# An expert gather ring of eight buffers in place of ten, and a weight slot that keeps two query pieces, then two output pieces

## What is computed

```python
def _peer(x, w_pq, sub_keys, u, v):
    q = (xt @ w_pq).reshape(T, PEER_HEADS, 2, PEER_HALF)
    scores = jnp.einsum('thcd,hckd->thck', q, sub_keys)
    ...   # top 16 of each half, top 16 of the 256 sums, per head: 8 * 16 = 128 experts a token
    def block(args):
        u_sel = jnp.take(u, idb, axis=0)          # 128 rows of 1024 for each token
        h = jax.nn.gelu(jnp.einsum('td,ted->te', xblk, u_sel), approximate=False)
        v_sel = jnp.take(v, idb, axis=0)
        return jnp.einsum('te,ted->td', gb * h, v_sel)
```

## Time and profile before

| what | value |
|---|---|
| median of 3 runs (lowest to highest) | 2794.46 us (2789.7 to 2795.59) |
| profiled execution | 2794.93 us |
| its span from first to last instruction | 2793.1 us |
| TensorE busy / DVE / ACT / POOL, share of the span | 90% / 62% / 35% / 24% |
| gathers, first issue to last issue | 134.7 to 1569.6 us |
| bytes moved by DMA | 800.03 MB, 536.93 of them by the gathers |
| granted TensorE clock, mean | 0.982 |

### The profile page before, as it was taken

One profiled execution on the slowest core, in us unless ns is written; L12 is line 12 of the kernel. 1 busy time (PEld: TensorE's weight loads), 2 busy tenths in 40 slices (PEclk: granted clock), 3 DMA queues, 4 the chain that ended last, 5 costly groups with the idle time before them and its releaser, 6 DMA issues.

```text
span 2793.1 us, 29435 instructions
## 1 busy us (share of the span) xinstructions
PE 2508.8 (90%) x9845; PEld 1561.3 (56%) x9845; DVE 1737.3 (62%) x3951; ACT 974.6 (35%) x2020; POOL 665.7 (24%) x635
## 2 busy tenths in 40 slices
PE   7989888798887899887877899999999999999999
PEld 3544444364442565432322356885688668875787
DVE  1678866755758666667776457653566556546664
ACT  1225322234222354222221234442444444424543
POOL 0044433433434334434444201001000020002000
PEclk9999999999999999999999999999999999999999
DMA  7299999999999999999999732544054325533352
GB/s 290 107 407 421 412 421 418 421 421 413 408 421 422 416 394 393 420 415 422 421 421 418 314 122 84 202 148 198 34 213 175 131 83 184 193 117 121 144 188 104
DMA packets 112145, 800.03 MB, mean 286 GB/s; under 512 B 13123, under 2 KB 15766, under 8 KB 19606
## 3 DMA queue, kind: packets, MB, share of 16 engines
q0 software_dynamic: 73760, 536.93, 46.6%
q1 hardware_dynamic: 38262, 261.60, 24.7%
HBM read 797.41 MB, written 1.07 MB: 286 GB/s over the span
## 4 chain that ended last, share of the span: by engine, by line
PE 63%; DMA 24%; DVE 7%; issue 3%; ACT 2%; SPq 1%; POOL 0%; DVEq 0%; ACTq 0%
PE psum L1343 15%; DMA weights<-in_peer_uv,scratch 13%; PE psum L1451 13%; PE psum L1074 11%; DMA arena<-in_peer_uv,scratch 9%; PE psum L1408 8%; PE psum L1410 4%; PE psum L1160 3%; PE psum L1168 2%; DVE heads_arena L2269 2%; PE psum L1146 1%; PE psum L1057 1%; PE psum L1135 1%; PE psum L1122 1%; ACT scratch L1781 1%
## 5 line engine op out<-in xcount | busy, mean ns | idle before, releaser
L1343 PE MATMUL psum<-weights,scratch 128*128 128x512 f32 x1232 | 589.4, 625 | 146.7 <-ACT scratch L1781 146.5
L2774 POOL DMA_INDIRECT weights<-in_peer_uv,scratch x308 | 356.0, 1156 | 608.4 <-PE psum L1343 503.3
L1343 PEld LDWEIGHTS psum<-weights,scratch 128*128 128x128 f32 x1232 | 234.1, 198 | 472.2 <-issue 249.6
L1343 PE MATMUL psum<-arena,scratch 128*128 128x512 f32 x816 | 383.3, 614 | 78.3 <-ACT scratch L1781 78.2
L2618 DVE TENSOR_TENSOR piece<-weights,piece 128x2048 fp32r<-128x2048 f32 x128 | 292.1, 2292 | 181.4 <-ACT piece L1860 181.4
L1074 PE MATMUL psum<-weights,xT 128*128 128x512 f32 (+2 forms) x792 | 338.2, 581 | 25.5 <-DMA weights<-in_w_qkv_a 15.2
L1451 PE MATMUL psum<-piece,hidden 128*128 128x512 f32 x1536 | 358.9, 390 | 0.0
L1773 ACT ACTIVATE scratch<-scratch 128x2 f32<-128x2 f32 x256 | 51.9, 203 | 844.0 <-DVE heads_arena L2269 843.8
L1408 PE MATMUL psum<-split_x,piece 128*128 128x512 f32 x896 | 318.6, 398 | 0.0
L1451 PEld LDWEIGHTS psum<-piece,hidden 128*128 128x128 f32 x1536 | 284.3, 188 | 59.6
L1343 PEld LDWEIGHTS psum<-arena,scratch 128*128 128x128 f32 x816 | 152.4, 194 | 286.2 <-issue 159.1
(11 more groups left out here) (266 smaller groups left out, 2779.1 us busy)
## 6 DMA issues: line engine op xcount, KB each, us to landing
weights<-in_w_up SPq DMA_DIRECT2D x64, 1024.0 KB, 4.9
weights<-in_w_down SPq DMA_DIRECT2D x64, 1024.0 KB, 4.8
weights<-in_w_kv_b SPq DMA_DIRECT2D x16, 1024.0 KB, 9.0
weights<-in_peer_w_q SPq DMA_DIRECT2D x12, 1024.0 KB, 9.1
weights<-in_a_w_in SPq DMA_DIRECT2D x6, 2048.0 KB, 10.2
weights<-in_w_q_b SPq DMA_DIRECT2D x8, 1024.0 KB, 9.4
weights<-in_w_o_b SPq DMA_DIRECT2D x8, 1024.0 KB, 9.2
weights<-in_a_w_out SPq DMA_DIRECT2D x4, 2048.0 KB, 8.9
```

Source lines behind the costliest of these rows:

```text
L1343: mm = pe.matmul(psum[g.bank][:, :], diagonal[:, n % DIAGONALS, :], row[:, D + half * BANK:D + (half + 1) * BANK], start=(k == 0), stop=(k ...
L2774: pool.indirect_dma_start(gathered[n % GATHER_SLOTS], None, rows, bass.IndirectOffsetOnAxis(ap=expert[:, w % NT, k:k + 1], axis=0), elemen ...
```

## The change

The ring has eight buffers. Weight slot 3 is no longer part of it. It holds, one after the other, what the kernel has in it anyway and another chunk of the same size. The first is `peer_chunks[1]`, columns 512 to 1023 of the first layer's query weight, which is loaded before the gathers begin, for tile 0. `Second` now uses its two halves in pairs 49 and 50 of pass 0 in place of two pieces of its own (`KeptPiece`). The other is `kept_o`, the first 512 columns of `w_o_b`, 2 MB, loaded once in pass 1 behind the layer norm's gains and used in pairs 35 and 36 of passes 1 and 2. The remaining two output pieces of these passes stay pieces of slot 0. `early_in` exchanges the slots of its chunks 1 and 2, so that chunk 1 goes to slot 3.

```diff
-GATHER_SLOTS = 10
+GATHER_SLOTS = 8
...
-        in_slot = {slot: [weights[:, slot, n * ROW:(n + 1) * ROW] for n in range(2)] for slot in (1, 2, 3)}
-        gathered = in_slot[2] + in_arena + in_slot[1] + in_slot[3]
+        in_slot = {slot: [weights[:, slot, n * ROW:(n + 1) * ROW] for n in range(2)] for slot in (1, 2)}
+        gathered = in_slot[2] + in_arena + in_slot[1]
...
-                self.loaded = 16 * half_uses[self.half]
+                self.landed = (piece_loaded[self.half], 16 * half_uses[self.half])
...
+        class KeptPiece:
+            def __init__(self, c, n, bank):
+                self.landed = (c.sem, c.loaded)
+                self.view = c.halves[:, n]
+                self.group = group(bank)
...
-                self.peer_q = [Piece(src, n, 2 + n % 2) for n, src in enumerate(column_pieces(A["peer_w_q"][0], 0))]
+                self.peer_q = [Piece(src, n, 2 + n % 2) for n, src in enumerate(column_pieces(A["peer_w_q"][0], 0)[0:2])]
+                self.peer_q += [KeptPiece(peer_chunks[1], n, 2 + n) for n in range(2)]
...
-                self.o = [Piece(src, first + n, banks[n % 2]) for n, src in enumerate(column_pieces(A["w_o_b"][0], 0))]
+                self.o = [KeptPiece(kept_o, n, banks[n]) for n in range(2)]
+                self.o += [Piece(src, first + n, banks[n]) for n, src in enumerate(column_pieces(A["w_o_b"][0], 0)[2:4])]
...
-        ring_free = {0: diff_out_blocks[1][-1], 2: later_blocks[4][-1], 4: later_blocks[5][-1], 6: later_blocks[1][-1], 8: peer_q[1]}
+        ring_free = {0: diff_out_blocks[1][-1], 2: later_blocks[4][-1], 4: later_blocks[5][-1], 6: later_blocks[1][-1]}
...
+        kept_o = in_weights(A["w_o_b"][0], 0, 3, second.peer_q[3].group)
...
-        for slot, buffers in ((1, (6, 7)), (2, (0, 1)), (3, (8, 9))):
+        kept_until = stick[1].o[1].group
+        slot_release[3] = (psum_filled[kept_until.bank], kept_until.filled)
+        for slot, buffers in ((1, (6, 7)), (2, (0, 1))):
...
-        early_in = TileProjection(chunks_laid_out(A["a_w_in"][0], A_IN), (0, 2, 3, 1), (0, 1, 2, 3))
+        early_in = TileProjection(chunks_laid_out(A["a_w_in"][0], A_IN), (0, 3, 2, 1), (0, 1, 2, 3))
...
-            load_stick(second.peer_q[2:])
             scored = second.scores[3]
...
                 load_ln(2 if s.t == 0 else 4)
+                if s.t == 0:
+                    load_chunks([kept_o])
                 load_stick(s.pieces[2:])
-                load_stick(s.o)
+                load_stick(s.o[2:])
```

More of the change, by code:

```diff
@@ L1150, in piece_loaded_to @@
             def piece_loaded_to(c):
-                pe.wait_ge(piece_loaded[c.half], c.loaded)
+                pe.wait_ge(*c.landed)
                 bank_free(c.group)
```

## The result

| | median us | lowest to highest | profiled execution | its span |
|---|---|---|---|---|
| before | 2794.76 (4 runs) | 2789.7 to 2795.59 | 2794.93 | 2793.1 |
| after | 2819.66 (4 runs) | 2814.35 to 2820.68 | 2820.68 | 2818.9 |

After is to before as 1.0081, with a 95% interval of 1.0064 to 1.0099. The kernel became 0.8% slower, 24.9 us by the medians. I had forecast 2797.3 and a range up to 2808, so the time lies 12 us above the range.

The account below looks back on a forecast made before the run. DMA was taken to bound most of the first 1600 us, with short stretches set by TensorE or DVE. Terms 2.0 + 1.8 + 1.6 + 5.0 - 4.0 - 1.9 - 1.7 = +2.8 us gave 2797.3, range 2786 to 2808.

Parts of the forecast that it names:

- part 1: Two buffers fewer: gathers late only where old issue of n + 2 plus 5.5 us passes n's old landing; clean stretches lose zero.
- five places: Where the release test failed: start, pair 34 and pair 55 of pass 0, and the output pieces of passes 1 and 2.
- Start of pass 0: Gather 8 lands up to 3.6 us late, a DMA gap behind it takes up part; +2.0 us.
- Pair 34: Pass 0, behind the norm's steps on DVE: a gather 2.0 us late; +1.8 us, ends 0 and 2.0.
- Query pieces and pair 55: Pass 0: 5.0 us of DMA from two unloaded pieces is spent by the smaller ring; +1.6 us, ends -5.0 and +2.0.
- The kept chunk: Output chunk loaded early in pass 1, near pair 7, where DMA is full; +5.0 us, other end 0.
- Output pieces of pass 1: Two pieces not loaded; 4.7 of 5.0 us can be had, less the query pieces' share; -4.0 us, ends -5.0 and -2.0.
- Pass 2: Two output pieces not loaded; 2.6 us to be had, less late gathers and a query piece; -1.9 us, ends -5.0 and 0.
- Last pass: No added delay: clean stretch stays at 421 GB/s, with issue to landing 9.1 us in place of 14.1.
- Chunk 1: Next input projection's chunk, issued when the last gather lands, 9 us before, removes TensorE's wait; -1.7 us.
- the bytes count in full: Rival: 4 MB fewer fetches save 10.0 us and the ring costs nothing, 2782.8; half or more of it, chance 0.18.
- The starving ring: Rival: clean pairs starve too if a gather behind one other needs over 8.3 us; 2800 and up, chance 0.32.

Follow-up runs that it names:

- ring9: The kernel before with nine gather buffers in place of ten and nothing else; 2799.11 us, ratio 1.0010.
- ring8: The kernel before with eight gather buffers, slot 3 empty during the gathers, all query and output pieces loaded as before; 2825.11 us, ratio 1.0105.
- after_weigh_first: The kernel after with VectorE weighing pair i - 1 before the products of pair i, and ScalarE's diagonals moved ahead likewise; 2789.95 us, ratio to before 0.9971.
- ring6: The kernel before with six gather buffers, one execution; 3286.44 us.
- ring10_hold8: The kernel before with all ten buffers, but GpSimd waits for the mix of gather n - 8 before issuing gather n; 2823.59 us, ratio 1.0086.
- the kernels with the new order: Pair i - 1 weighed ahead of pair i's products: kernel after 2789.95 us, kernel before 2790.49, eight buffers without kept pieces 2793.06, nine with half a slot kept 2786.54.
- after_late_kept: The kernel after with the 2 MB output chunk loaded behind the twelve pieces of pass 1, some 28 pairs later; 2819.99 us, ratio 1.0099.
- ring8_output: The kernel after with the output pieces kept but all query pieces loaded as before; 2821.54 us, ratio 1.0082.

## Why the prediction was wrong, step by step

The forecast was +2.8 us on the profiled execution, and it became +25.8. Of the 23.0 us between, 4.0 arose in pass 0, 2.7 in pass 1, 8.3 in pass 2, 1.6 in the last pass and 6.4 behind the last pass's gathers (chunk 1 included).

The failing step is the test of part 1, "old issue of n + 2, plus 5.5, against the old landing of n", and the sentence that it fails in five places. It went wrong in two ways.

First, I had run it only where I was looking. Over all 512 gathers of the kernel before, the same test with the same 5.5 us fails for 53. Beside my places it fails in pairs 34 to 37 of pass 1, by up to 1.7 us, and in pairs 23 to 39 of pass 2, by up to 6.2. I had no term for these, and put pass 2 at -1.9 where it was +6.4.

Second, 5.5 us is the landing of a gather with nothing ahead, and the test takes the releases at their old times. At my five places, the gathers of the kernel after that it was meant for took 5.7 us (start of pass 0), 6.2 (pair 34), 8.6 and 10.8 (the two of pair 55), 9.0 and 7.9. So the floor was about right at the first two, and 2.4 to 5.3 us too short at the other three. At the two places where I counted on a saving that ate 3.5 of the 4.7 us to be had in pass 1, and 2.4 of the 2.6 in pass 2.

The other half of part 1, "in clean stretches DMA stays full", held for this kernel (420 GB/s, 5.04 us a pair), though not for the same ring without the kept pieces; that stands under the last pass below.

How thin the reserve became can be counted. Every 0.1 us from the first mix to 30 us before the last I took how many gathers were between the start of their issue and their last completion signal, and summed the bytes of all DMA packets in those times. Each cell has the us and, where these are ten or more, the GB/s:

| in flight | before | ring9 | ring8 | after | after_weigh_first | ring6 |
|---|---|---|---|---|---|---|
| 1 | 1 | 2 | 14, 238 | 15, 283 | 5 | 431, 202 |
| 2 | 23, 381 | 58, 358 | 145, 372 | 176, 359 | 46, 369 | 999, 340 |
| 3 | 88, 385 | 195, 393 | 708, 407 | 672, 408 | 208, 396 | 412, 367 |
| 4 | 184, 407 | 655, 417 | 532, 415 | 528, 418 | 483, 416 | 17, 356 |
| 5 | 633, 419 | 475, 420 | 33, 421 | 31, 423 | 526, 420 | 0 |
| 6 and 7 | 471, 421 | 24, 423 | 0 | 0 | 126, 422 | 0 |
| lost against 421.5 GB/s (us) | 22 | 30 | 56 | 56 | 30 | 509 |

The kernel before spent 1104 of its 1400 us at five or more in flight; the kernel after spends 31 there and 863 at three or fewer. (The ring of six also had 35 us with none.) Fewer in flight and a lower rate go together: five or six have 419 to 423 GB/s, three 367 to 408, two 340 to 381, one 202 to 283. But the number alone doesn't set the rate. At three it is 385 in the kernel before and 408 after, and in pairs 10 to 40 of the last pass the kernel after had three or four in flight and 417 at either. Where few are in flight because TensorE frees no buffer, the low rate is the consequence of a wait and not its cause.

The last row is the sum of (421.5 - rate) / 421.5 over all the time. It is a restatement and no test: it equals the time counted less the bytes divided by 421.5, so its differences are how much longer a kernel took, plus the bytes that it saved. Ring 8 loses 34 us more than before by it and is 29.6 late; the rest comes from where the count begins and ends: the kernel before has 1.5 MB more inside it, and ring 8 starts its first mix 1.7 us earlier. A test would forecast one kernel from another. Shifting the time before by two gathers, with its own rates (ring 8's for one in flight), adds some 130 us, where two buffers cost 30; shifting it by one adds some 40, where one buffer cost 3 to 4. So the distribution shows that the reserve is gone, not what that costs. What it costs is shown by ring10_hold8 and the kernels with the new order.

The time of a gather by what was ahead of it at its issue gives the size of the second error. In the kernel after it is 6.5 us at the median with one gather ahead (17 of them), 8.3 with two (89) and 9.1 with three (344). In the ring of six, with none ahead, it is 5.9 (45). The Trainium skill, "DMA: Bandwidth & Descriptors", section "Anatomy of one DMA", has a fixed 2.0 us for a DMA issued from GpSimd and puts most of it behind the last byte. In the ring of six the first packet of a gather with nothing ahead started 1.9 us after its issue did, so here that much lies ahead of the first byte, and the measurement decides. The formula of the Trainium skill there makes an estimate of 4.4 us for the whole gather, which would have made my sum still smaller; the shortest landing in the ring of six was 5.3.

Now term by term, at the mixes of the kernel after:

- **Start of pass 0, predicted +2.0: +4.0 at pair 10**, beyond the upper end of 3.6. The test was near for the first gather: number 8 went out at 158.97, took 5.7 us and landed 3.0 later than in the kernel before. But the DMA gap behind it, which I had counted on to take up a part, grew instead: 349 GB/s at 160 to 180 us in place of 372. Once late, the gathers stayed late. The chain there has one that was released at 176.44 and took 13.1 us, as it took 13.4 in the kernel before, since the pass's pieces are loaded just then:

```profile
176.19 0.26 issue
176.44 13.08 DMA weights<-in_peer_uv,scratch
189.53 0.02 issue
189.55 1.25 DVE heads_arena L2283 x2
```

  I had taken the same pieces as a reason for the lower half. They didn't help; the gathers share DMA with them in both kernels.
- **Pair 34, predicted +1.8: from +4.3 at pair 33 to +6.4.** Right in place and near in size; +3.9 was the level from pair 26 to 30, so up to 2.5.
- **Query pieces and pair 55, predicted +1.6: +3.9**, from 5.5 at pair 47 to 9.4. I had seen that the 5.0 us of the saved loads would be lost, and the stretch at 314 GB/s shows it. The lateness at pair 55 was more than twice what the test gave: its two gathers took 8.6 and 10.8 us from their issue, with two and three ahead of them, and not 5.5.
- **The kept chunk, predicted +5.0: +5.3 at pair 9 of pass 1.** Right in size. The step is gone in after_late_kept and back in ring8_output, which has the early load (+6.0 from pair 7 to 9). But ring8, without that load, went 3.2 us later there in its one profiled execution, so a part can be the ring.
- **Output pieces of pass 1, predicted -4.0: -1.2** from pair 34 to the end. With ten buffers the saved loads brought 6.4 us in this pass; with eight the ring took most of it. This was the first large error: the earlier trace rows show when the gather could be released, but it took 9.0 us from there, with two gathers ahead, in place of 5.5.
- **Pass 2, predicted -1.9: +6.4.** Of this +4.1 arose between pairs 29 and 34, and +4.0 between pairs 46 and 55, of which 1.4 went back by the last pair. The first is where the test fails by up to 6.2 us and I hadn't looked. Two things of 1.7 to 1.8 us each can be read there. The mix of pair 30 took 5.40 us in place of 3.70, in a stretch with a granted clock of 0.91. And pair 34 waited for a gather that a late mix released:

```profile
1090.55 5.40 PE psum L1357 x8
...
1098.54 1.73 PE psum L1357 x4
1100.27 0.26 issue
1100.53 1.90 POOL weights L2788
1102.43 0.30 issue
1102.73 7.61 DMA weights<-in_peer_uv,scratch
```

  The sign that I had named came: the gap at 1040 to 1110 us is wider. The stretches of 20 us from 1040 had 391, 363, 381 and 423 GB/s before, and 379, 376, 365 and 380 after.
- **Last pass, predicted 0: +1.6.** Nearly right for this kernel; the chain has the 9.1 us that I forecast. Yet the same ring lost 5.6 us here in ring8 and 9.1 in ring10_hold8. In both, stretches with a low granted clock have low DMA rates (0.84 with 379 GB/s at 1360 us in ring8, 0.83 with 359 at 1340 in ring10_hold8). The kernel before has such a stretch too, and there DMA stays full. From 1320 to 1340 us, first the kernel before, then ring8; the last three columns are the granted clock, DMA's share and GB/s:

```profile
1320.00:1340.00 20.00, 15.30 (x31) 6.04 (x30) 15.85 (x45) 7.50 (x18) 7.77 (x8) 0.91 1.01 420
1320.00:1340.00 20.00, 16.00 (x33) 6.33 (x32) 16.01 (x40) 7.07 (x18) 10.22 (x8) 0.91 1.00 390
```

  So "clean stretches stay full" holds with eight buffers only as long as nothing delays a mix; with ten, a mix may be 1.7 us late and DMA doesn't show it. The low clock isn't why the kernel after is slower as a whole: from its first mix to its last the granted clock has a mean of 0.974, and 0.971 in the kernel before.
- **Chunk 1, predicted -1.7: -2.0**, from +21.2 at the last mixes to +19.2. Right; TensorE goes on without a wait:

```profile
1613.58 7.03 PE L1614 MATMUL psum<-heads_arena,const 128*128 128x512 f32 x16
1620.45 7.03 PE L1088 MATMUL psum<-weights,xT 128*128 128x512 f32 x16
```

- **Behind that, predicted 0: +6.6 in the profiled execution**, in five steps, one of -1.6 and four of +0.9 to +2.9. The two nearest follow the granted clock. The kernel before had 0.91 at 1620 to 1640 us, where it lost 1.6 us to the kernel after; the kernel after has it later. First the one row of the kernel before, then two of the kernel after:

```profile
core 0: us, PE busy (x) PEld busy (x) DVE busy (x) ACT busy (x) POOL busy (x), PEclk, DMA share, GB/s
1620.00:1640.00 20.00, 18.55 (x73) 11.36 (x72) 10.53 (x47) 5.06 (x18) 0.00 (x0) 0.91 0.00 0
...
1640.00:1660.00 20.00, 18.38 (x80) 10.99 (x78) 10.79 (x47) 5.53 (x19) 0.00 (x0) 1.00 0.29 105
1660.00:1680.00 20.00, 17.31 (x71) 11.05 (x72) 9.78 (x43) 9.86 (x35) 7.44 (x16) 0.91 0.42 159
```

  Since the kernels of the table swing from -6.6 to +5.5 us between the end of pass 3 and the span's end, I don't put this on the change. That is argued, not shown, and it leaves some 6 us of the 24.9 without a cause in the passes.

Of the rivals, "the bytes count in full" is out. The starving ring came nearest in time, but its mechanism did not hold for this kernel: it put the cost on clean pairs with a threshold at 8.3 us, and the clean pairs landed in 9.0 and kept 5.04 us a pair against 5.02. In ring8 and ring10_hold8 the pairs of the last pass took 5.10 and 5.16, so something of it was there. What it had in a half sentence, "a share of this, from DVE's or POOL's delays of 1 to 2 us that ten buffers hid", fits what happened, and I priced it at 4 us. The steps that I followed stand where VectorE, a piece, a norm or a slow mix holds the mixes up for a moment.

My accounting of part 1 also had the slope wrong. From ten buffers to nine 2.5 us of reserve go and cost some 3 us; from nine to eight 2.5 more go and cost 26. I had reckoned both as if on the flat part.

What stays open: how the cost divides between the places, beyond single profiled executions that differ by some us; and why the rate is lower with two gathers in flight. In the kernel before the sixteen completion signals of one gather came over 4.4 us at the median, so the engines don't finish it together, and a new gather brings nothing for its first 1.9 us. Both fit, and no run takes them apart.

## What to carry to other kernels

Before a prefetch ring is made smaller, run the release test over every transfer and not only where trouble is expected, and take for the landing what a transfer takes with others ahead of it (8 to 9 us here, not 5.5). How well the test then forecasts a time no run here shows. Hold the transfers back by one wait before anything is rebuilt: that one edit, ring10_hold8, measures what the smaller ring costs. A load that is saved beside a ring need not be worth its bytes: here 10 to 11 of 15 us came through with ten buffers, and with eight 5.5 of 10 by the medians, which the intervals don't settle. And reserve can be had without memory: one step moved ahead in two engines' order gave back what the two buffers had given.

## What the runs showed of the hardware that I had not expected

- Two indirect gathers of 1 MB in flight had 340 to 381 GB/s, where five had 419 to 423 (the kernels of the table above). Three had 367 to 408 over the whole, and 417 in a stretch without disturbance. One alone takes 5.9 us at the median, of which the first 1.9 move nothing.
- A loop that starves TensorE pays twice: in the last pass of the ring of six 30 of 64 mixes took over 5 us in place of 3.7, in a stretch with a granted clock of 0.79, and a loop of two pairs took 14.9 us where landing and a full clock would make 13.5.
- The same dip of the granted clock, 0.91 over 20 us, left DMA at 420 GB/s with ten buffers and at 390 with eight (1320 to 1340 us).
- The same code behind the gathers took up to 7 us more or less in total from one profiled execution to another, while the places of the difference were few and each 1 to 3 us.
